# Two row blocks in one scores visit, and each pair's projection work in four runs, in a hybrid attention and SwiGLU layer

## What is computed

```python
def rms_norm(x, gain):
    xf = x.astype(jnp.float32)
    xf = xf * lax.rsqrt(jnp.mean(xf * xf, axis=-1, keepdims=True) + RMS_EPS)
    return (xf * gain.astype(jnp.float32)).astype(x.dtype)
...
    def qblock(i):
...
        s = jnp.einsum('bhmqd,bhmkd->bhmqk', qb, k).astype(jnp.float32) * scale
        mask = k_pos[None, :] <= (start + jnp.arange(QB))[:, None]
        p = jax.nn.softmax(jnp.where(mask, s, -jnp.inf), axis=-1)
        a = p[:, :, 0] - lam * p[:, :, 1]
        return jnp.einsum('bhqk,bhkd->bhqd', a.astype(v.dtype), v)
...
        h = rms_norm(x, attn_norm[l])
        proj = jnp.einsum('bsd,de->bse', h, w_in[l])
        mq, mk, mv, dq, dk, dv = jnp.split(proj, splits, axis=-1)
...
        moba_out = moba_attention(mq, mk, mv)
...
        diff_out = diff_attention(dq, dk, dv, lam)
        diff_out = rms_norm(diff_out, diff_subln[l]) * (1.0 - lambda_init)
...
        x = x + jnp.einsum('bse,ed->bsd', mixed, w_out[l])

        h = rms_norm(x, ffn_norm[l])
        g = jnp.einsum('bsd,df->bsf', h, w_gate[l])
        u = jnp.einsum('bsd,df->bsf', h, w_up[l])
        x = x + jnp.einsum('bsf,fd->bsd', jax.nn.silu(g) * u, w_down[l])
```

## Time and profile before

| | us |
|---|---|
| median of 3 runs | 617.97 |
| lowest, highest | 617.85, 619.09 |
| the profiled execution | 617.75 |
| its span, first to last instruction | 615.9 |
| TensorE busy | 599.6 (97%) |
| VectorE busy | 476.8 (77%) |
| ScalarE busy | 312.5 (51%) |

### The profile page before, as it was taken

How to read it: one execution, slowest core, us unless ns; L and a number is a source line. 1 busy time by engine, 2 the same in 40 slices (tenths; PEclk the granted TensorE clock), 3 DMA queues, 4 the chain that set the end, 5 groups by cost and what they waited for, 6 DMA issues and landing times.

```text
span 615.9 us, 10356 instructions
## 1 busy us (share of the span) xinstructions
PE 599.6 (97%) x3774; PEld 514.5 (84%) x3774; DVE 476.8 (77%) x785; ACT 312.5 (51%) x535; POOL 28.1 (5%) x28
## 2 busy tenths in 40 slices
PE   6999999999999999999999999999999999999997
PEld 5866677676768676879999999999999998888886
DVE  4867767687777878687877887788777877999774
ACT  6354546373554454544744554445544555555551
POOL 0000000000000000000000000000000012145200
PEclk9999999999999999999999999999999999999999
DMA  8413031221404041504403332234223459699901
GB/s 324 114 46 115 10 128 48 88 72 65 131 7 138 6 167 66 191 17 140 151 21 134 138 101 95 81 137 137 69 74 133 138 133 263 190 192 206 196 36 68
DMA packets 32954, 70.31 MB, mean 114 GB/s; under 512 B 3345, under 2 KB 3729, under 8 KB 32913
## 3 DMA queue, kind: packets, MB, share of 16 engines
q1 hardware_dynamic: 26608, 58.14, 28.1%
q0 software_dynamic: 6016, 11.54, 10.6%
q10 hardware_dynamic: 288, 0.08, 0.1%
HBM read 63.45 MB, written 2.10 MB: 106 GB/s over the span
## 4 chain that ended last, share of the span: by engine, by line
PE 89%; DVE 6%; ACT 2%; issue 2%; DMA 1%; DVEq 0%; ACTq 0%
PE ps L1484 26%; PE ps L1486 25%; PE ps L1485 25%; PE ps L1548 3%; PE ps L1561 2%; PE ps L1516 2%; PE ps L1578 1%; DVE w_lo L968 1%; ACT probs L620 1%; DVE w_lo L950 1%; PE ps L1586 1%; DMA ident<-ident 1%; PE ps L1807 1%; PE ps L1625 1%; DVE residual L1216 0%
## 5 line engine op out<-in xcount | busy, mean ns | idle before, releaser
L1484 PE MATMUL ps<-h_sum_parts,w_hi 128*128 128x256 f32 x432 | 121.1, 280 | 0.7 <-ACT q_kept L810 0.7
L1486 PE MATMUL ps<-h_sum_parts,w_lo 128*128 128x256 f32 x432 | 120.5, 279 | 0.0
L1485 PE MATMUL ps<-h_sum_parts,w_hi 128*128 128x256 f32 x432 | 120.5, 279 | 0.0
L1484 PE MATMUL ps<-h_parts,w_hi 128*128 128x512 f32 x192 | 81.3, 423 | 1.4 <-DVE h_parts L1082 1.0
L1484 PEld LDWEIGHTS ps<-h_sum_parts,w_hi 128*128 128x128 f32 x432 | 81.1, 188 | 0.9 <-ACT q_kept L810 0.9
L1486 PEld LDWEIGHTS ps<-h_sum_parts,w_lo 128*128 128x128 f32 x432 | 81.2, 188 | 0.0
L1485 PEld LDWEIGHTS ps<-h_sum_parts,w_hi 128*128 128x128 f32 x432 | 80.8, 187 | 0.0
L1486 PE MATMUL ps<-h_parts,w_lo 128*128 128x512 f32 x192 | 75.4, 393 | 0.0
L1485 PE MATMUL ps<-h_parts,w_hi 128*128 128x512 f32 x192 | 75.0, 391 | 0.0
L620 ACT ACTIVATE probs<-ps,small 128x128 f32<-128x128 f32 (+3 forms) x64 | 39.0, 614 | 51.2 <-DVE small L1031 51.2
L1484 PE MATMUL ps<-w_hi,hidden_parts 128*128 128x512 f32 x154 | 59.9, 389 | 0.0
(11 more groups left out here) (179 smaller groups left out, 1241.1 us busy)
## 6 DMA issues: line engine op xcount, KB each, us to landing
w_raw<-wt SPq DMA_DIRECT2D x61, 512.0 KB, 4.3
w_raw_odd<-wt SPq DMA_DIRECT2D x24, 512.0 KB, 4.3
w_raw_odd<-wt POOLq DMA_DIRECT2D x12, 512.0 KB, 7.6
down_raw<-wt SPq DMA_DIRECT2D x6, 512.0 KB, 10.1
w_raw<-wt POOLq DMA_DIRECT2D x5, 512.0 KB, 10.2
residual<-x SPq DMA_DIRECT2D x4, 512.0 KB, 5.5
q_rotated<-q_gained SPq DMA_DIRECT2D x32, 64.0 KB, 2.0
k_rotated<-k_gained SPq DMA_DIRECT2D x32, 64.0 KB, 2.0
```

The costliest lines, as they stand in the source:

```text
L1484: nc.tensor.matmul(dst, lh, rh, start=start, stop=False, skip_group_check=True)
L1485: nc.tensor.matmul(dst, lh, rl, start=False, stop=False, skip_group_check=True)
L1486: return nc.tensor.matmul(dst, ll, rh, start=False, stop=stop, skip_group_check=True)
```

## The change

A pair has three scores visits and not four: VISITS = ((0, 1), (2,), (3,)). The first computes row blocks 0 and 1 together: block 1 lies in columns 0 to 255 of banks 2 and 3 and block 0 in columns 256 to 383, so that the two diagonal blocks lie side by side, and one instruction of 512 elements adds the mask to both. Maxima stay one instruction per row block; the bias, the inverted sums and the differential factor are made for both blocks at once. For MoBA pairs the turned probabilities of block 0 go to columns 384 to 511 of banks 4 and 5, and turn_p(t, 1) follows turn_p(t, 0) at once.

On TensorE the units come in four runs for each pair, 6, 5, 6 and 7 (pair 0: 2, 5, 5, 5 and 7; pair 7: 6, 5, 6 and 4). Behind the last run, spread_k, both parts of heads_out, the next pair's scores(t+1, 0) and turn_v(t+1) stand in one stretch, the last two ahead of the loop's end. On VectorE project_lo(t+1, 2) and v_scale come ahead of norm(t, 0), and project_lo(t+1, 4) ahead of k_rope in all pairs (it stood behind k_norm in most). On ScalarE project_hi(t+1, 2) comes ahead of the pair's first exps. Number and columns of the matmuls are the same as before.

```diff
 WARM = 4
+VISITS = ((0, 1), (2,), (3,))
+NV = len(VISITS)
+def score_at(qt):
...
+        def turned_at(qt, moba):
+            return 3 * P if moba and qt == 0 else 0
...
+            def exps(t, v, moba):
+                act.wait_ge(nb_s, t * NV + (v + 1))
+                for qt in VISITS[v]:
+                    W = (qt + 1) * P
+                    at = score_at(qt)
+                    for a in range(2):
+                        i = 2 * qt + a
+                        if qt >= 2:
+                            act.wait_ge(pt_s, turned(t, qt - 2, a, moba))
+                        elif from_(t, 1):
+                            moba_before = t - 1 < MOBA_PAIRS if isinstance(t, int) else moba
+                            act.wait_ge(pt_s, turned(t - 1, qt + 2, a, moba_before))
+                        nc.scalar.activation(PR[qt % 2][:, a, 0:W], ps[:, 2 + a, at:at + W], ACT.Exp,
+                                             bias=NB[:, i:i + 1], scale=RQ[:, i:i + 1],
+                                             accum_out=SUM[:, i:i + 1]).then_inc(ex_s, 1)
...
                 for a in maps(moba):
-                    act.wait_ge(pt_s, turned(t, qt, a, moba))
+                    act.wait_ge(pt_s, turned(t, max(qt, 1) if moba else qt, a, moba))
                     if from_(t, 1):
                         act.wait_ge(pv_s, t)
-                    bank = 4 + (a if moba else qt % 2)
+                    bank, at = 4 + (a if moba else qt % 2), turned_at(qt, moba)
                     nc.scalar.activation(PT[:, a, 0:qt + 1, qt * P:(qt + 1) * P],
-                                         ps[:, bank, 0:(qt + 1) * P].rearrange("p (k q) -> p k q", q=P),
+                                         ps[:, bank, at:at + (qt + 1) * P].rearrange("p (k q) -> p k q", q=P),
                                          ACT.Copy).then_inc(pt_ev, 1)
...
             with act.Fori(1, MOBA_PAIRS) as t:
+                project_hi(t + 1, 2)
                 exps(t, 0, True)
+                exps(t, 1, True)
                 pt_copy(t, 0, True)
-                exps(t, 1, True)
-                project_hi(t + 1, 2)
-                project_hi(t + 1, 3)
-                exps(t, 2, True)
                 pt_copy(t, 1, True)
                 q_evac(t + 1, False)
-                exps(t, 3, True)
+                project_hi(t + 1, 3)
+                pt_copy(t, 2, True)
+                exps(t, 2, True)
                 k_evac(t + 1, False)
-                pt_copy(t, 2, True)
                 pt_copy(t, 3, True)
                 project_hi(t + 1, 4)
                 v_evac(t + 1)
...
+            def maxima(t, v):
+                n = t * NV + (v + 1)
+                first, blocks = VISITS[v][0], len(VISITS[v])
+                i = slice(2 * first, 2 * (first + blocks))
+                at = P if v == 0 else first * P
+                diagonal = ps[:, 2:4, at:at + blocks * P].rearrange("p a (b k) -> p a b k", b=blocks)
                 dve.wait_ge(sc_s, n)
-                nc.vector.tensor_tensor(diagonal, diagonal, mask[:].unsqueeze(1).broadcast_to([P, 2, P]),
+                nc.vector.tensor_tensor(diagonal, diagonal,
+                                        mask[:].unsqueeze(1).unsqueeze(1).broadcast_to([P, 2, blocks, P]),
                                         ALU.add).then_inc(masked, 1)
                 dve.wait_ge(masked, n)
-                nc.vector.tensor_reduce(MX[:, i], ps[:, 2:4, 0:W], AX.X, ALU.max).then_inc(mx_s, 1)
+                for qt in VISITS[v]:
+                    s0 = score_at(qt)
+                    ins = nc.vector.tensor_reduce(MX[:, 2 * qt:2 * qt + 2], ps[:, 2:4, s0:s0 + (qt + 1) * P], AX.X,
+                                                  ALU.max)
+                ins.then_inc(mx_s, 1)
                 dve.wait_ge(mx_s, n)
                 dve.wait_ge(rq_s, t + 1)
                 nc.vector.scalar_tensor_tensor(out=NB[:, i], in0=MX[:, i], scalar=-1.0, in1=RQ[:, i], op0=ALU.mult,
                                                op1=ALU.mult).then_inc(nb_s, 1)
...
+            def norm(t, v, moba):
+                first, blocks = VISITS[v][0], len(VISITS[v])
+                i, last = 2 * first, 2 * (first + blocks)
+                dve.wait_ge(ex_s, t * 8 + last)
+                nc.vector.reciprocal(RS[:, i:last], SUM[:, i:last]).then_inc(rs_s, 1)
+                dve.wait_ge(rs_s, t * NV + (v + 1))
+                if not moba:
+                    nc.vector.scalar_tensor_tensor(out=NL[:, first:first + blocks], in0=SUM[:, i:last:2], scalar=MLAM,
+                                                   in1=RS[:, i + 1:last:2], op0=ALU.mult,
+                                                   op1=ALU.mult).then_inc(lr_s, 1)
+                    dve.wait_ge(lr_s, t * NV + (v + 1 - NV * MOBA_PAIRS))
+                for qt in VISITS[v]:
+                    W = (qt + 1) * P
+                    p0, p1 = PR[qt % 2][:, 0, 0:W], PR[qt % 2][:, 1, 0:W]
+                    if moba:
+                        nc.vector.tensor_scalar(p0, p0, RS[:, 2 * qt:2 * qt + 1], None, ALU.mult).then_inc(pn_s, 1)
+                        nc.vector.tensor_scalar(p1, p1, RS[:, 2 * qt + 1:2 * qt + 2], None,
+                                                ALU.mult).then_inc(pn_s, 1)
+                    else:
+                        nc.vector.scalar_tensor_tensor(out=p0, in0=p1, scalar=NL[:, qt:qt + 1], in1=p0, op0=ALU.mult,
+                                                       op1=ALU.add).then_inc(pn_s, 1)
+                if not moba and v == NV - 1:
+                    sums = SUM.rearrange("p (t a) -> p t a", a=2)[:, :, 0]
+                    nc.vector.scalar_tensor_tensor(out=EO, in0=sums, scalar=EPS, in1=sums, op0=ALU.mult,
+                                                   op1=ALU.mult).then_inc(eo_s, 1)
...
             with dve.Fori(MOBA_PAIRS + 1, PAIRS - 1) as t:
                 maxima(t, 0)
+                project_lo(t + 1, 2)
+                v_scale(t)
                 norm(t, 0, False)
                 maxima(t, 1)
-                v_scale(t)
-                project_lo(t + 1, 2)
+                o_norm(t - 1)
                 norm(t, 1, False)
                 maxima(t, 2)
-                o_norm(t - 1)
-                maxima(t, 3)
+                project_lo(t + 1, 3)
                 norm(t, 2, False)
-                norm(t, 3, False)
                 mix_lo(t - 1, False)
-                project_lo(t + 1, 3)
                 q_rope(t + 1)
                 scales(t + 1)
+                project_lo(t + 1, 4)
                 k_rope(t + 1)
                 k_norm(t + 1)
...
+            def scores(t, v):
+                first = VISITS[v][0]
+                if v == 0:
                     pe.wait_ge(q_step, t * 3 + 3)
                     pe.wait_ge(kn_s, t + 1)
-                if from_(t, 1) or qt >= 1:
-                    pe.wait_ge(ex_s, t * 8 + 2 * qt)
+                if from_(t, 1) or v >= 1:
+                    pe.wait_ge(ex_s, t * 8 + 2 * first)
                 rows = (slice(0, HEAD), slice(HEAD, P))
-                for a in range(2):
-                    ins = nc.tensor.matmul(ps[:, 2 + a, 0:W], QF[rows[a], qs], KF[rows[a], 0:W], start=True,
-                                           stop=True, skip_group_check=True)
+                for qt in VISITS[v]:
+                    W = (qt + 1) * P
+                    at = score_at(qt)
+                    for a in range(2):
+                        ins = nc.tensor.matmul(ps[:, 2 + a, at:at + W], QF[rows[a], qt * P:W], KF[rows[a], 0:W],
+                                               start=True, stop=True, skip_group_check=True)
                 ins.then_inc(sc_s, 1)
...
                     pe.wait_ge(pn_s, n)
-                    if from_(t, 1) or qt >= 1:
+                    if moba and qt == 1:
+                        if from_(t, 1):
+                            pe.wait_ge(pt_ev, n - 4)
+                    elif from_(t, 1) or qt >= 1:
                         pe.wait_ge(pt_ev, n - 2)
-                    bank = 4 + (a if moba else qt % 2)
+                    bank, at = 4 + (a if moba else qt % 2), turned_at(qt, moba)
                     for kt in range(qt + 1):
-                        ins = nc.tensor.transpose(ps[:, bank, kt * P:(kt + 1) * P],
+                        ins = nc.tensor.transpose(ps[:, bank, at + kt * P:at + (kt + 1) * P],
                                                   PR[qt % 2][:, a, kt * P:(kt + 1) * P], ident[:])
                     ins.then_inc(pt_s, 1)
...
             with pe.Fori(1, MOBA_PAIRS) as t:
                 fill = filler(t + 1)
-                fill(1)
-                scores(t, 0)
-                fill(2)
-                turn_v(t)
-                fill(1)
+                fill(6)
                 scores(t, 1)
                 turn_p(t, 0, True)
-                fill(4)
+                turn_p(t, 1, True)
+                fill(5)
                 scores(t, 2)
-                fill(4)
-                turn_p(t, 1, True)
```

(31 more changed lines are left out.)

198 lines of the change are left out of this document (64 added, 134 removed).

## The result

The changed kernel takes 609.1 us (608.8 to 609.25, 4 runs) against 617.91 (617.62 to 619.09, 4 runs) for the kernel before beside it: ratio 0.9853, interval 0.9836 to 0.987, which is 8.8 us or 1.5% faster. The forecast was 610.5 with a range of 609.0 to 614.0. The direction came out, and the waits mostly as they were walked; the price of the merged visit and of a break did not, and the gain was larger than forecast: 609.1 is only 0.1 inside the range.

A forecast was written before the change was run, and what follows sets the result against it. TensorE, busy 97% of the span, was taken as the bound. Gains of 1.6 (pair 1), 1.2 (2, 3), 0 (4), 1.0 (5), 2.2 (6) and 1.5 (7) made 7.5 us: 617.75 to 610.25, median 610.5, range 609.0 to 614.0.

The forecast's parts named there:

- the price of the merged visit and of a break: TensorE, each pair: merged scores visit stays 1.06 us; a break costs 0.17 ahead of 64-row scores, otherwise 0.11.
- The walk: Pair-by-pair timing of the attention part: period 27.3 us in MoBA pairs, 26.8 in pair 4, 26.5 in pairs 5 and 6.
- The first leg: From heads_out's end to the second scores visit: TensorE's 5.83 us covers an exps chain of 5.88, waiting some 0.05.
- H: The moment heads_out ends, where each pair's period starts; forecast 27.3 us from one to the next in MoBA pairs.
- k_ready: Rival at pair boundaries: k_norm late, TensorE waits at seven boundaries, 9.2 us at the worst wait, 619.7; chance 0.07.
- S1: A pair's second scores visit, ending the first leg; wait for exps there forecast near zero.
- Half a microsecond at S1: Sign against the forecast: the second scores visit waiting half a microsecond or more in each pair.
- the sum: Gains over pairs 1 to 7, 7.5 us in all; 0.62 us of breaks removed for each MoBA pair.
- pair 4: First differential pair: pure TensorE 25.6 us plus 1.1 of waits, given as 26.8, no gain on 26.78.
- The chain to k_norm: VectorE's work from mean_squares to k_norm, visible 20.1 us after the second scores visit, 1.3 ahead of need in MoBA pairs.
- The longer visit-0 chain: Rival in the first leg: exps chain outlasts six units, 0.4 us more in each of eight pairs, 613.5; chance 0.17.
- Breaks cost nothing that can be removed: Rival on TensorE's unit runs: some 5 us of the 7.5 fall, only the waits go, 615.5; chance 0.10.

The follow-up runs named there:

- e1: The changed kernel with the merged scores visit in two pieces, turn_v between them: 613.34 us, ratio 0.9916.
- e2: The changed kernel with one unit from the run ahead put between the two parts of heads_out: 610.78 us, ratio 0.9877.
- e9: The changed kernel with three breaks put back in each pair, two ahead of turns, one between heads_out's parts: 610.9 us, ratio 0.9883.
- e5: The changed kernel with a MoBA pair's mix_lo moved behind the maxima of the next pair's second visit: 606.17 us; run again, 608.21 us.
- e10: e5 with, in pair 4, seven units ahead of the last turn and six behind, instead of six and seven: 606.48 us, ratio 0.9812.
- e4: The changed kernel with project_lo(t + 1, 4) put back behind k_norm(t + 1) on VectorE: 608.3 us, ratio 0.9852.
- e3: The changed kernel with spread_k between the two parts of heads_out, no unit there: 610.75 us, ratio 0.9872.
- e6: The kernel before with TensorE's list alone changed: five runs of units, one joined stretch, four scores visits: 638.11 us, ratio 1.031.
- e8: e5 with the low part of output tile 27 ahead of mix_lo(6) in pair 7: 606.59 us, ratio 0.9809.

## Where the prediction was right, and the step that failed

**The walk held.** The first leg was forecast as a balance of 5.83 against 5.88 and came as 5.91 with exps at H + 3.78 and recip at H + 5.89. The exps' side was right, TensorE's was not: without the wait it needs 5.56 to 5.64, since the merged visit is shorter, and so waits 0.27 in pairs 2 and 3, not 0.05. No wait for k_ready came, as forecast: k_norm is visible at S1 + 20.2 (walked: 20.1) and H at S1 + 21.3 (21.4). Half a microsecond at S1, the mark that would have refuted the walk, was not reached.

**The step that failed: the price of the merged visit and of a break.** The prediction said a merged visit stays at 1.06 "since the cost goes with columns and weight loads, not with visits", and charged breaks by their number and not by the tile shapes on both sides. Measured: 0.86, and 0.19 for each change of shape (e1, e2), 0.01 for a break without one in e2's differential pairs and at most 0.05 in e9's pair 2. The rows for it were in the trace of the kernel before: visits of one to four blocks show 0.21 for each 128 columns and 0.21 on top, and I read only the largest. A MoBA pair goes from twelve changes of shape to seven, 5 x 0.19 = 0.95, where the sum had 0.62 less 0.1.

Checked against the pairs: without any wait (e5) a MoBA pair is 26.85, that is 1.03 less than the 27.88 before, which had none either. A differential pair loses only two changes, 0.37, since its heads' output has the units' shape. Here the count is short: pair 4 without waits is 25.67 (e10) against 26.24 before (26.78 less 0.33 and 0.21 of waits), that is 0.57 less. The 0.2 beyond the two changes would be some 0.05 for each of the four other breaks that went, an estimate that no run took apart. Over all pairs the timelines show 80 changes of shape from the first spread_k to the end of pair 7 before and 52 now: 28 x 0.19 = 5.3 of the 9.5 us. Most of the rest are waits that went; the named ones in that stretch fell by 4.0, but shorter ones are in neither list.

At this place the prediction had weighed a rule of the Trainium skill (TensorEngine Tiling (Array Packing), Key Properties), that a change of tiling mode drains TensorE, and left it out of the sum. The traces agree with it better than with my count of breaks: e2's one break costs 0.35 where the shape differs and 0.01 where it does not. The 0.19 is from the rows of e1 and e2; they show what a change costs, not what TensorE does in that time.

**Where the surplus lies.** The attention part gained 2.0 more than forecast: 0.6 in pair 0, 0.6 in pairs 1 to 3, 0.15 in pair 4, 0.1 each in pairs 5 and 6, and 0.5 in pair 7. The merged visit is 0.2 cheaper than forecast in all eight, 1.6 together, and in pairs 1 to 3 the heads' output in one piece brings another 0.2 each (2.30 instead of 1.66 + 0.85). Against that stand the waits for exps in pairs 2 and 3, and in the differential pairs the other breaks, which gave less than they were charged: pair 4 without waits is 25.67 where the forecast had 25.6 with the dearer visit. So the near hit in pairs 4 to 6 is two errors that cancel, and in part luck. The rest of the surplus is waits set too high: pair 0 waited 0.23 and 0.20 instead of 0.4 and 0.5, and pair 7 0.40 instead of 0.75. The later start of that one execution, 1.05, hid half of the surplus in the time.

**Slips in the sums.** Pair 4 is 25.6 + 1.1 = 26.7, not 26.8. The chain to k_norm adds up to S1 + 19.96, not 20.1. And the breaks cannot be both "about half" of the 7.5 and the 5 us that the rival takes from it. None of them decides anything.

**The rivals.** The longer visit-0 chain: it exists, at 0.27 in pairs 2 and 3, and e5 shows that VectorE's mix_lo is all of it there (pair 0, which has no mix_lo ahead of it, waits 0.23 behind only five units). "Breaks cost nothing that can be removed": half true. As to turns it was right, and as to scores and to the heads' output of MoBA pairs it was wrong, because these change the shape. k_ready: absent in the changed kernel and in e4; with less cover, in e3, it is there with 0.17 at three boundaries. And e6 shows a way to be slower that the prediction did not have, though not for this change: a like order on TensorE, with four scores visits and without the moves on VectorE and ScalarE, is 3.1% slower.

## What to carry over

Count the changes of tile shape on TensorE, not the places where a run of matmuls is interrupted: here each change costs 0.19 us, and work of the units' own shape may be put between them for 0.01 to 0.05. When the order of the busiest engine is changed, look at what it reads on the other engines too: with their lists left as they were, the waits and the lower clock cost more than the joins gave (e6). And where a leg has no slack, look at what the engine behind it does first: one 0.69 us operation moved out of the way was worth 0.1 to 0.35 us in pairs 1 to 3 and 0.46 in pair 4.

## What the runs showed of the hardware beyond that

TensorE's granted clock can fall from 2.4 to 1.2 GHz behind a stretch that hardly shows as idle: 0.31 us of waiting, four turns and 16 two-column matmuls, then a fall for 3.5 us inside a run of 512-column matmuls, worth 1.6 us, in three of the ten profiles that have this wait in pair 4 (e1, e5, e8), and not in the one without it (e10). The fall came 2.4 to 2.7 us behind the wait's end. In e6 the same wait of 1.06 us stands at this place in pairs 1, 2 and 3, and the clock fell behind that of pair 2 alone. So what decides whether it falls is not shown by these runs. The 32 turns of x at the start took 4.2 to 5.8 us at a granted clock of 1.00, with no edit near them; what sets it was not tried.
